# Eight score units take over half of the second filling gate chunk of a hybrid RWKV-7 / MLA block

## What is computed

```python
u = rms_norm(h, norm_mix); proj = u @ w_in          # 1024 x (1824 + 416 + 2048)
z_rwkv, c_q, c_kv, k_rope, gate_a, gate_b = split(proj)
y_a = rwkv7_branch(token_shift(z_rwkv), ...)
y_b = mla_branch(c_q, c_kv, k_rope, ...)            # 8 heads, causal softmax attention
merged = sigmoid(gate_a) * y_a + sigmoid(gate_b) * y_b
h = h + merged @ w_out
h = h + square(relu(rms_norm(h) @ w_ff_up)) @ w_ff_down
return rms_norm(h)
```

## Time and profile before

| | us |
|---|---|
| median of 3 runs (lowest, highest) | 1509.39 (1509.32, 1513.35) |
| the profiled execution, its own time | 1510.3 |
| its span from first to last instruction | 1508.6 |
| attention's matmuls, from the first scores to the last product with V | 110.8 to 253.3 |
| the filling chunk after it, to the first window's first matmul | 253.3 to 263.0 |

### The profile page before, as it was taken

One profiled execution on the slowest core, in us unless ns is written; L12 is line 12 of the kernel. 1 busy time (PEld: TensorE's weight loads), 2 busy tenths in 40 slices (PEclk: granted clock), 3 DMA queues, 4 the chain that ended last, 5 costly groups with the idle time before them and its releaser, 6 DMA issues.

```text
span 1508.6 us, 24973 instructions
## 1 busy us (share of the span) xinstructions
PE 1475.5 (98%) x9685; PEld 1216.7 (81%) x9685; DVE 1045.0 (69%) x1658; ACT 683.2 (45%) x1232; POOL 132.4 (9%) x163
## 2 busy tenths in 40 slices
PE   6999999999999999999999999999999999999998
PEld 5987888777777888887787878888888887888887
DVE  6566764568687582679865489777777757777785
ACT  6555664244433213656313246444444433333453
POOL 1013320000010001364000020000000000000000
PEclk9999999999999999999999999999999999999999
DMA  5031002722222536204446115444443699889754
GB/s 193 15 80 43 16 16 64 223 69 70 83 76 61 168 126 154 86 4 138 133 160 240 53 58 175 153 153 153 151 149 136 229 327 326 279 277 306 269 179 151
DMA packets 181115, 216.53 MB, mean 144 GB/s; under 512 B 28789, under 2 KB 115186, under 8 KB 180242
## 3 DMA queue, kind: packets, MB, share of 16 engines
q1 hardware_dynamic: 180942, 215.11, 43.7%
q10 hardware_dynamic: 68, 0.02, 0.0%
HBM read 156.20 MB, written 56.92 MB: 141 GB/s over the span
## 4 chain that ended last, share of the span: by engine, by line
PE 82%; DVE 9%; ACT 3%; DMA 2%; issue 2%; SPq 0%; ACTq 0%; DVEq 0%
PE bank L3115 20%; PE bank L3516 20%; PE bank L3580 13%; PE bank L3422 4%; PE bank L3481 4%; PE bank L3013 3%; PE bank L3025 2%; PE bank L3040 2%; PE bank L2969 2%; PE bank L2902 2%; PE bank L3050 2%; DVE down_raw L2717 1%; DVE hacc L2757 1%; PE bank L3611 1%; DMA wc_raw<-in_w_in 1%
## 5 line engine op out<-in xcount | busy, mean ns | idle before, releaser
L3115 PE MATMUL bank<-uT_hi,w_hi 128*128 128x512 f32 x432 | 170.8, 395 | 0.0
L3115 PE MATMUL bank<-uT_hi,w_lo 128*128 128x512 f32 x432 | 168.2, 389 | 0.0
L3115 PE MATMUL bank<-uT_lo,w_hi 128*128 128x512 f32 x432 | 168.2, 389 | 0.0
L3580 PE MATMUL bank<-mg_lo,mg_hi 128*128 128x512 f32 x576 | 135.0, 390 | 0.5 <-DVE mg_hi L2724 0.5
L3580 PEld LDWEIGHTS bank<-mg_lo,mg_hi 128*128 128x128 f32 x576 | 107.8, 188 | 24.3 <-DVE mg_hi L2724 2.0
L3580 PE MATMUL bank<-yh,mg_lo 128*128 128x512 f32 x384 | 118.5, 390 | 0.2 <-DVE mg_lo L2724 0.2
L1421 ACT ACTIVATE zbuf<-bank 128x512 f32<-128x512 f32 x54 | 32.2, 598 | 173.5 <-PE bank L3115 169.2
L1788 ACT ACTIVATE f<-f 128x512 f32<-128x512 f32 x64 | 40.5, 632 | 131.6 <-DVE f L2682 69.7
L3115 PEld LDWEIGHTS bank<-uT_hi,w_hi 128*128 128x128 f32 x432 | 81.1, 188 | 21.9 <-issue 5.2
L3115 PEld LDWEIGHTS bank<-uT_hi,w_lo 128*128 128x128 f32 x432 | 81.1, 188 | 17.4 <-issue 1.0
L3115 PEld LDWEIGHTS bank<-uT_lo,w_hi 128*128 128x128 f32 x432 | 81.1, 188 | 16.9
(11 more groups left out here) (515 smaller groups left out, 3783.1 us busy)
## 6 DMA issues: line engine op xcount, KB each, us to landing
down_raw<-in_w_ff_down SPq DMA_DIRECT2D x80, 512.0 KB, 4.8
down_raw<-f_spill SPq DMA_DIRECT2D x56, 512.0 KB, 4.8
f_spill<-x SPq DMA_DIRECT2D x80, 256.0 KB, 2.9
w_raw<-in_w_in SPq DMA_DIRECT2D x28, 512.0 KB, 4.2
sgate<-gate_spill SPq DMA_DIRECT2D x16, 512.0 KB, 4.4
up_a<-in_w_ff_up SPq DMA_DIRECT2D x16, 512.0 KB, 5.0
up_b<-in_w_ff_up SPq DMA_DIRECT2D x16, 512.0 KB, 4.1
f_spill<-f SPq DMA_DIRECT2D x32, 256.0 KB, 2.2
```

The lines of the kernel that those rows point to most:

```text
L3115: ins = nc.tensor.matmul(ps[2 * slot + g][:], st[:, slot, k, :], mv[:, k, g * HALF:(g + 1) * HALF], start=(k == 0 and m == 0), stop=(k == ...
L3580: ins = nc.tensor.matmul(ps[4 * (q % 2) + t][:], st, mv_, start=(start and w == 0 and m == 0), stop=(stop and w == 1 and m == 2))
```

## The change

`fw_raw[1]` moves to the place that `wide` has, and is loaded ahead of attention. `wide` is made later, by GpSimd, after the low parts of split 6. The rounding of the weights moves on ScalarE from u = 24 to u = 18. Their low part moves from VectorE to GpSimd, behind `k_low(5)`. The first half of chunk 8, 24 matmuls, goes in threes into steps 21 to 28, ahead of the transposes, into bank 3, and ScalarE copies it out at u = 30 without the sigmoid. After the loop only the second half's 24 matmuls are left, 6 ahead of the last product with V and 18 behind it. ScalarE takes the sigmoid of the first half, from and to `fz`, after `round_w(0)`. The diff, cut to its core:

```diff
+LATE_FILL, LATE_UNITS = 16, 8
-        fw_hi, fw_raw1 = place(179, ("fw_hi", [P, KD, P], F32R), ("fw_raw1", [P, KD, P], F32))
+        fw_hi, = place(179, ("fw_hi", [P, KD, P], F32R))
+        fw_raw1, = place(191, ("fw_raw1", [P, KD, P], F32))
...
                 # SP
                 sp.dma_start(fw_raw[0][:], win[:, :, GATE0 + P:GATE0 + 2 * P]).then_inc(s_wc, 16)
+                sp.wait_ge(s_rd, 16 * (1 + 16))
+                sp.dma_start(fw_raw[1][:], win[:, :, GATE0 + KD * P:GATE0 + (KD + 1) * P]).then_inc(s_fw1.sem, 16)
...
                 sp.dma_start(gate_dram[1], fz[:]).then_inc(s_eg, 16)
-                sp.wait_ge(s_eg, 32)
-                sp.dma_start(fw_raw[1][:], win[:, :, GATE0 + KD * P:GATE0 + (KD + 1) * P]).then_inc(s_wc, 16)
...
                 # GpSimd
-                pool.wait_ge(s_rd, 16 * (1 + 16))
-                pch(pool, nc.gpsimd.memset(wide[:], 0.0))
-                nc.gpsimd.affine_select(out=wide[:, T - P:T], ...).then_inc(s_cst2, 1)
...
                 for n in range(2, 2 * NT):
                     q_low(n)
                     k_low(n)
+                    if n == LATE_FILL // 4 + 1:
+                        pool.wait_ge(s_wch, KD + 3)
+                        nc.gpsimd.tensor_tensor(fw_lo[:], fw_raw[1][:], fw_hi[:].bitcast(F32), ALU.subtract).then_inc(s_wcl, 1)
+                        pool.wait_ge(s_wcl, KD + 3)
+                    if n == LATE_FILL // 4 + 2:
+                        pch(pool, nc.gpsimd.memset(wide[:], 0.0))
+                        nc.gpsimd.affine_select(out=wide[:, T - P:T], ...).then_inc(s_cst2, 1)
...
                 # ScalarE, attention's loop
-                    if u == 3 * NH:
+                    if u == LATE_FILL + 2:
                         round_fill(1)
+                    if u == LATE_FILL + 6 + LATE_UNITS:
+                        act.wait_ge(s_eg, 32)
+                        evac_fill(1, 0, 3, ACT.Copy)
...
                 # ScalarE, after round_w(0)
                 for g in range(2):
-                    evac_fill(1, g, 2 + g, ACT.Sigmoid)
+                    if g == 1:
+                        evac_fill(1, 1, 3, ACT.Sigmoid)
+                    else:
+                        act.wait_ge(s_ce, NT + 5)
+                        nc.scalar.activation(fz[:, 0:HALF], fz[:, 0:HALF], ACT.Sigmoid).then_inc(s_ce, 1)
...
                 # VectorE, attention's loop
-                    if u == 3 * NH + 2:
-                        rest_fill(1)
...
                 # TensorE, attention's loop, ahead of transpose_probs(u)
+                    if LATE_FILL + 5 <= u < LATE_FILL + 5 + LATE_UNITS:
+                        if u == LATE_FILL + 5:
+                            pe.wait_ge(s_wcl, KD + 3)
+                            pe.wait_ge(s_ce, NT + 4)
+                        j = 3 * KD // LATE_UNITS * (u - LATE_FILL - 5)
+                        fill(3, 0, j, j + 3 * KD // LATE_UNITS)
...
                 # TensorE, after the loop
-                pe.wait_ge(s_wcl, KD + 3)
-                fill(2, 0, 0, 6)
+                fill(3, 1, 0, 6)
                 values(n)
...
                 nc.tensor.transpose(ps[4][0:NT * NH, 0:P], psums[:, 0, :], ident[:]).then_inc(s_rtr, 1)
-                fill(2, 0, 6, 3 * KD)
-                fill(3, 1, 0, 3 * KD)
+                fill(3, 1, 6, 3 * KD)
```

More of the change, by code:

```diff
@@ L605, in program @@
         s_hst = Again(s_spo, 16)
+        s_fw1 = Again(s_pos, 16)
         s_bt, s_bn = Again(s_vt, 2), Again(s_vcol, 1)
@@ L791, in _ @@
                     if w == 1:
-                        sp.wait_ge(s_ce, NT + 6)
+                        sp.wait_ge(s_ce, NT + 7)
                         sp.dma_start(gate_dram[KD], fz[:]).then_inc(s_eg, 16)
@@ L1066, in _ @@
                     nc.gpsimd.tensor_tensor(qr[:, j, :], rp_cos[:], rp_sin[:], ALU.add).then_inc(s_rs, 1)
-                pool.wait_ge(s_rd, 16 * (1 + 16))
-                pch(pool, nc.gpsimd.memset(wide[:], 0.0))
-                nc.gpsimd.affine_select(out=wide[:, T - P:T], in_=wide[:, T - P:T], compare_op=ALU.is_ge, fill=NEG, base=0,
-                                        pattern=[[-1, P]], channel_multiplier=1).then_inc(s_cst2, 1)
                 nc.gpsimd.memset(bones[:], 0.0).then_inc(s_bo, 1)
@@ L1101, in _ @@
                     k_low(n)
+                    if n == LATE_FILL // 4 + 1:
[4 more added lines that the diff above has]
+                        pch(pool, nc.gpsimd.memset(wide[:], 0.0))
+                        nc.gpsimd.affine_select(out=wide[:, T - P:T], in_=wide[:, T - P:T], compare_op=ALU.is_ge, fill=NEG, base=0,
+                                                pattern=[[-1, P]], channel_multiplier=1).then_inc(s_cst2, 1)
                 pool.wait_ge(s_pv, NT * NH // 2)
@@ L1320, in round_fill @@
                 def round_fill(n):
-                    act.wait_ge(s_wc, 16 * (3 + n))
+                    act.wait_ge(*((s_wc, 48) if n == 0 else s_fw1(16)))
                     act.wait_ge(s_cp, NT + 2 + 2 * n)
@@ L3073, in _ @@
                     if u == 4 * NH - 2:
-                        pe.wait_ge(s_ce, NT + 4)
+                        pe.wait_ge(s_ce, NT + 5)
                 n = NT * NH // 2 - 1
-                pe.wait_ge(s_wcl, KD + 3)
-                fill(2, 0, 0, 6)
+                fill(3, 1, 0, 6)
                 values(n)
@@ L3110, in half_chunk @@
                         pe.wait_ge(s_ze, 2 * (w - 2) + g + 1)
-                    elif w == 1:
-                        pe.wait_ge(s_ce, NT + 4 + g + 1)
+                    elif w == 1 and g == 1:
+                        pe.wait_ge(s_ce, NT + 6)
                     for k in range(KD):
```

## The result

The changed kernel's median is 1512.68 us over 17 runs, against 1509.58 for the kernel before over its 17; the ratio is 1.0017, with a 95% interval of 1.0009 to 1.0024 (it is estimated from all runs, so it is not quite the quotient of the two medians, 1.0021). A second set of 12 runs gave 1512.89 against 1509.77 and a ratio of 1.0012 (1.0002 to 1.0021). The profiled execution took 1513.68 us, with a span of 1512.0; before it was 1510.3 and 1508.6.

What follows compares the result with a forecast made beforehand. TensorE, busy for 98% of the span, was taken as the bound. Odd steps +3.20, even steps +1.02, rounding +0.43 and the end -2.54 gave +2.11 us: 1509.39 becomes 1511.5, range 1508.9 to 1513.4.

Steps and rivals of the forecast that it cites:

- the clock: Rival: clock halves in TensorE's new wait at attention's end, +5.4 us for 24 matmuls; chance 0.04, nothing in the sum.
- the sum: All terms for attention and its end added: +2.11 us, median 1509.39 becoming 1511.5.
- the interval given to the sum: Total time between 1510.4 and 1512.9 us if the summed terms hold; chance 0.68.
- The end: Attention's end: 24 matmuls leave, but the first window waits for its weights, so 2.54 us saved, not 5.46.
- The fill in attention: Three matmuls in each of steps 21 to 28: odd steps +3.20, even steps +1.02, together +4.22 us.
- the stall of step 26: Step 26: exponentials late because VectorE made the weights' low part first; moving that to GpSimd removes 0.42 us.
- an unfilled pair: Steps 28 and 29, without fill: TensorE waits 0.24 us in 3.82 us, all in the even step.
- The preparation: Rounding moved to u = 18 costs +0.43 us; low part moved to GpSimd removes step 26's stall, -0.42.
- The delay at step 18: Step 18: rounding ahead of the exponentials makes the transposes 0.57 us later, +0.43 us after a covered wait of 0.14.
- the wait for `k_low(5)`: Step 18: scores behind the transposes were held some 0.14 us by `k_low(5)`; the later transposes now cover this.
- GpSimd's queue: Low part on GpSimd takes 2.56 us and delays nothing: 0, with 1.4 us slack before the scores of unit 24.

Runs made afterwards that it cites:

- the run of the preparation alone: Kernel before with earlier load, rounding at u = 18, low part by GpSimd, later mask, all 48 matmuls still at the end: median 1509.68 us, ratio 0.9994.
- short_end: Kernel before with 23 of its last 24 filling matmuls left out and nothing changed in attention: median 1510.75 us, ratio 1.0004.

## Why the prediction was right, and where it wasn't

The direction and the range held: +2.1 us forecast, +2.6 (by the ratio) to +3.1 (by the medians) measured. Most of the mechanism held too, but the size holds in part by luck. Attention cost 0.5 us less than forecast, and the clock, which the sum had at nothing, cost 1.6 in the profile. With the terms as measured and without the clock the sum would be 4.15 - 2.40 = 1.75, that is 1511.3 on the median of 1509.58; the median of 1512.68 still lies in the interval given to the sum, but it got there through a rival that had a chance of 0.04.

*The end, forecast -2.54, measured -2.40.* Right but for 0.14 us: the window starts at 264.32 and the low part ends at 264.17, a step between the engines that the forecast left out. It is shown twice: cutting the matmuls without doing anything in attention gave the wait and no gain, and loading earlier gave the whole 5.4. A stage whose end is set by a load gives back only the slack of that load.

*The fill in attention, forecast +4.22, with the stall of step 26 inside.* Without it, as the run of the preparation alone allows to say, 4.64 was forecast and 4.37 measured. The three matmuls last as worked out (0.79 and 0.70). The 0.27 come from the transposes in odd steps: three behind fill take 0.25 (145.29 to 145.54) and not 0.30, four take 0.36 and not 0.41. So attention grew by 4.15 and not by the 4.65 that were forecast, the last product with V ended at 257.0 and not at 258.0, and the first window began at 264.3 and not at 265.1; 0.40 of each of these two differences stood ahead of attention already. The reading that decided it was the length of the wait in an unfilled pair: 0.24 of 3.82 us.

*The preparation, forecast +0.43 and -0.42, measured -0.22 in all.* The delay at step 18 is close to the forecast of 0.57 (from scores to transposes it took 0.99 and takes 1.50, 0.51 more), and covers the wait for `k_low(5)`. The stall of step 26 went as forecast, 0.42. What came on top is mostly at step 24, where the rounding had stood: I took it to cost nothing there, and it had cost 0.11 (1.09 against 0.98).

*GpSimd's queue, forecast 0.* Right: 2.38 us against 2.56, nothing held.

*The step that failed is the one on the clock.* The prediction gave it nothing in the sum, a chance of 0.04, and a price of 5.4 us for a whole half window. It happened in all four profiles of the changed kernel and cost 1.6 us in the first, and about as much in the others, whose windows took 23.45 to 23.67 against the 22.01 of the profile that kept the clock. The price was too high, because the clock came back after 3 to 3.4 us of matmuls; the chance was far too low. The Trainium skill ("TensorE: Matmul & The Clock Gate", section "Why this matters for your kernels") advises against gaps of about this length between bursts of matmuls and says that the clock goes back to half behind them. The profiles of the changed kernel agree, with 0.52 behind 2.85 us; the profile with a wait of 2.92 us and a clock of 1.00 does not, so here it is a risk and not a certainty.

The trace of the kernel before had a sign of it too, in rows that I didn't read. I argued from the clock's column, 1.00 before and after 11.3 us of near idleness. But the transposes right behind that idleness, 16 of them, from 15.3 to 18.5, load their weights in 230 ns at the median:

```profile
L2888 PEld LDWEIGHTS bank<-ident,xt x16: 177/230/230, 15.3 to 18.4; 128*128 128x128 f32 x16
```

and the same 16 at 33 us (both from one line's instructions of the kernel before, ns as min/median/max) in

```profile
L2888 PEld LDWEIGHTS bank<-ident,xt x16: 138/140/142, 32.9 to 34.6; 128*128 128x128 f32 x16
```

That alone could be something else, such as the transfers of that stretch. The second fall in `short_end` settles it, because transposes of the same size stand in it and, some 8 us earlier, at the full clock. The stretch, and one line's weight loads in it and ahead of it:

```profile
634.30:636.40 2.10, 2.10 (x22) 1.65 (x20) 0.86 (x2) 1.94 (x3) 0.00 (x0) 0.50 0.04 8
```

```profile
L3234 PEld LDWEIGHTS bank<-ident,zb x4: 183/227/230, 635.4 to 635.9; 128*128 128x128 f32 x4
...
L3234 PEld LDWEIGHTS bank<-ident,zb x4: 138/140/142, 627.7 to 628.0; 128*128 128x128 f32 x4
```

With the clock granted at 0.50 and hardly any transfers (8 GB/s) such a load takes up to 230 ns, at the full clock 140. By this pace TensorE ran at the lower level at 15.3 us, although the column said 1.00, and the earlier trace rows could not carry the argument that was built on them.

What stays open: why one execution loses the clock behind such a wait and another keeps it, and the 0.3 us by which the profiles differ behind the first window.

## What to carry to other kernels

Before work is moved off a stage's end, ask which chain sets that end next and how late it is: here it was a load that could be issued 6.4 us earlier, and without that edit more than half of what the end could give turned into a wait. Before work is moved into a loop, measure from start to start what a step without it waits, in each kind of step: 0.24 us in every second one is room for one matmul, not for three in each. And a wait of TensorE of the length seen here, 2.4 to 2.9 us, often had a price of its own, 1.6 us. Taking the cause of the wait away gave 4.5 us. Filling it with matmuls that nobody needs kept the clock, but left the window where it was.

## What the runs showed of the hardware that I had not expected

TensorE that waits 2.4 to 2.9 us can lose the full clock, here in five of six profiles with such a wait. The fall came between 0.4 us ahead of the end of the wait and 1.3 us behind it, and 3 to 3.4 us of matmuls ran at the low clock, where matmuls of 512 columns follow each other after 0.43 us and not 0.23. With a wait of 6.66 us it was 5.3 us of matmuls. The same kernel can keep the clock in one execution and lose it in the next. In one profile twelve matmuls into a bank that nobody reads kept the clock, and of the runs of that kernel one of 11 had a mean clock below 0.999, against 13 of 17. The clock's column can't be relied on at the start of a program: it showed 1.00 while weights loaded in 230 ns, which elsewhere goes with a granted clock of 0.50, and which take 140 ns at the full one.
